# One-hot vectors weighted by their gates on ScalarE instead of VectorE, in an encoder block with dense and sparse expert retrieval

## What is computed

```python
def peer_ffn(x, w_pq, sub_keys1, sub_keys2, peer_u, peer_v):
    ...
    v1, i1 = lax.top_k(s1, PEER_TOPK)
    v2, i2 = lax.top_k(s2, PEER_TOPK)
    ...
    top_s, pos = lax.top_k(cand_s, PEER_TOPK)
    idx = jnp.take_along_axis(cand_i, pos, axis=-1)
    gate = jax.nn.softmax(top_s, axis=-1).astype(x.dtype)
    ...
        u_sel = jnp.take(peer_u, ib, axis=0)
        act = jax.nn.gelu(jnp.einsum('thkd,td->thk', u_sel, xb), approximate=False) * gb
        v_sel = jnp.take(peer_v, ib, axis=0)
        return jnp.einsum('thk,thkd->td', act, v_sel)
```

## Time and profile before

| what | value |
|---|---|
| median of 3 runs | 3290.34 us (3289.21 to 3291.01) |
| profiled execution, its own time | 3295.16 us |
| its span in the profile | 3293.5 us |
| PE busy | 3119.8 us (95%) |
| DVE busy | 2073.9 us (63%) |
| ACT busy | 367.9 us (11%) |
| POOL busy | 682.0 us (21%) |
| mean DMA rate over the span | 313 GB/s |

### The profile page before, as it was taken

One profiled execution on the slowest core, in us unless ns is written; L12 is line 12 of the kernel. 1 busy time (PEld: TensorE's weight loads), 2 busy tenths in 40 slices (PEclk: granted clock), 3 DMA queues, 4 the chain that ended last, 5 costly groups with the idle time before them and its releaser, 6 DMA issues.

```text
span 3293.5 us, 27033 instructions
## 1 busy us (share of the span) xinstructions
PE 3119.8 (95%) x10342; PEld 1889.4 (57%) x10342; DVE 2073.9 (63%) x2874; ACT 367.9 (11%) x653; POOL 682.0 (21%) x557
## 2 busy tenths in 40 slices
PE   8999998899999898999989999999999999999797
PEld 5444443334445577678874447884458853478443
DVE  5356532342668779889997766656566666656675
ACT  1233212320101211112210000000000000000000
POOL 0000000000021134322222333222222333223240
PEclk9999999999999999999999999999999999999899
DMA  6222221047797678998998999999999999999985
GB/s 267 77 77 70 86 65 44 10 166 261 294 408 309 258 316 358 417 387 305 350 350 350 389 422 421 421 415 417 421 421 421 419 419 416 422 421 421 412 368 233
DMA packets 152515, 1029.69 MB, mean 313 GB/s; under 512 B 16464, under 2 KB 21712, under 8 KB 35664
## 3 DMA queue, kind: packets, MB, share of 16 engines
q0 software_dynamic: 78512, 557.88, 41.6%
q1 hardware_dynamic: 73888, 470.24, 36.4%
HBM read 1007.08 MB, written 20.97 MB: 312 GB/s over the span
## 4 chain that ended last, share of the span: by engine, by line
DMA 41%; PE 33%; DVE 18%; issue 4%; ACT 2%; POOL 2%; DVEq 0%; SPq 0%; ACTq 0%; POOLq 0%
DMA arena<-peer_v,arena 40%; PE ps L693 10%; DVE arena L1750 7%; PE ps L1077 4%; PE ps L845 3%; DVE arena L1788 2%; DVE arena L1739 2%; PE ps L935 2%; PE ps L863 2%; PE ps L770 1%; PE ps L1050 1%; PE ps L799 1%; ACT arena L1117 1%; POOL arena L611 1%; PE ps L785 1%
## 5 line engine op out<-in xcount | busy, mean ns | idle before, releaser
L1077 PE MATMUL ps<-arena 128*128 128x512 f32 x2048 | 884.8, 595 | 52.8 <-DVE arena L1800 52.0
L1050 PE MATMUL ps<-arena 128*128 128x256 f32 x4096 | 898.3, 381 | 9.6 <-ACT arena L1333 8.9
L1050 PEld LDWEIGHTS ps<-arena 128*128 128x128 f32 x4096 | 778.7, 191 | 118.9 <-ACT arena L1333 9.7
L1750 DVE SCALAR_TENSOR_TENSOR arena<-arena 128x2048 f32<-128x2048 f32 x256 | 601.8, 2351 | 298.8 <-DMA arena<-peer_v,arena 233.1
L1739 DVE CUSTOM_DVE_ANT_0 arena<-arena 128x2048 f32<-128x2048 f32 x256 | 586.2, 2290 | 288.4 <-DMA arena<-peer_u,arena 286.8
L1077 PEld LDWEIGHTS ps<-arena 128*128 128x128 f32 x2048 | 390.6, 191 | 544.8 <-issue 490.6
L611 POOL DMA_INDIRECT arena<-peer_u,arena x256 | 346.8, 1354 | 1108.3 <-DVE arena L1739 909.3
L622 POOL DMA_INDIRECT arena<-peer_v,arena x256 | 309.2, 1208 | 755.0 <-DVE arena L1750 725.8
L693 PE MATMUL ps<-arena 128*128 128x512 f32 x800 | 345.2, 592 | 1.1 <-ACT arena L1117 1.1
L693 PEld LDWEIGHTS ps<-arena 128*128 128x128 f32 x800 | 151.9, 190 | 192.2 <-issue 192.2
L1117 ACT ACTIVATE arena<-ps 128x512 f32<-128x512 f32 (+3 forms) x247 | 145.2, 611 | 774.9 <-PE ps L855 138.8
(11 more groups left out here) (179 smaller groups left out, 1804.9 us busy)
## 6 DMA issues: line engine op xcount, KB each, us to landing
arena<-peer_ut SPq DMA_DIRECT2D x128, 1024.0 KB
arena<-peer_vt SPq DMA_DIRECT2D x128, 1024.0 KB
arena<-w_row SPq DMA_DIRECT2D x52, 1024.0 KB
arena<-w_mix SPq DMA_DIRECT2D x48, 1024.0 KB
arena<-w_once SPq DMA_DIRECT2D x74, 512.0 KB, 3.5
arena<-w_feat SPq DMA_DIRECT2D x20, 1024.0 KB
dense_gates<-arena SPq DMA_DIRECT2D x8, 2048.0 KB, 7.3
arena<-dense_gates POOLq DMA_DIRECT2D x11, 1024.0 KB, 24.2
```

The lines of the kernel that those rows point to most:

```text
L1050: last = pe.matmul(ps[:, (e // 2) % 4, (e % 2) * DT:(e % 2 + 1) * DT], w[:, kt * P:(kt + 1) * P], XTD[:, kt * DT:(kt + 1) * DT], start=(kt ...
L1077: last = pe.matmul(bank(4 + (c % 2) * 2 + tb), G[:, t * DT + tb * P:t * DT + (tb + 1) * P], w[:, i * 512:(i + 1) * 512], start=(t == 0), s ...
L1750: dve.scalar_tensor_tensor(out=acc, in0=VB[e], scalar=AV[r // 4 % 2][:, r % 4:r % 4 + 1], in1=acc, op0=ALU.mult, op1=ALU.add).then_inc(v_f ...
```

## The change

The multiplication by the gates goes from one VectorE instruction (128x512) to four ScalarE instructions (128x128 each, in place, with one token's column of gates as the scale of each partition). VectorE's comparison now signals a new semaphore `hots_found`, and ScalarE signals `hots_ready`. ScalarE's list has the groups 0 and 1 ahead of the stage, and group n+2 right behind `stage_gates(n)`. VectorE no longer waits for its own comparison.

```diff
@@ one-hot stage, semaphores
-        hots_ready, oh_mm = sem("hots_ready"), sem("oh_mm")
+        hots_found, hots_ready, oh_mm = sem("hots_found"), sem("hots_ready"), sem("oh_mm")
@@ ScalarE
+            def gate_hots(n):
+
+                act.wait_ge(hots_found, n + 1)
+                for i in range(4):
+                    hot = OH[n % 2][:, i * NK:(i + 1) * NK]
+                    t = 2 * DT + 4 * n + i
+                    last = act.activation(hot, hot, ACT.Copy, scale=TB[:, t:t + 1])
+                last.then_inc(hots_ready, 1)
@@ ScalarE, the stage
             t = ONEHOT_FROM // 2 * 2 - 2
+            gate_hots(0)
+            gate_hots(1)
             for n in range(DT // 4):
                 if n % 8 == 1:
                     gelu_dense(0, t)
@@
                 stage_gates(n)
+                if n + 2 < DT // 4:
+                    gate_hots(n + 2)
@@ VectorE, one_hot_vectors
-                link(dve.tensor_tensor(oh, IOTA.unsqueeze(1).unsqueeze(1).broadcast_to([P, 2, 4, NK]),
-                                       turn[:, 0:2, here].unsqueeze(3).broadcast_to([P, 2, 4, NK]), ALU.is_equal))
-                dve.tensor_tensor(oh[:, 0], oh[:, 0], turn[:, 2, here].unsqueeze(2).broadcast_to([P, 4, NK]), ALU.mult
-                                  ).then_inc(hots_ready, 1)
+                dve.tensor_tensor(oh, IOTA.unsqueeze(1).unsqueeze(1).broadcast_to([P, 2, 4, NK]),
+                                       turn[:, 0:2, here].unsqueeze(3).broadcast_to([P, 2, 4, NK]), ALU.is_equal
+                                  ).then_inc(hots_found, 1)
```

## The result

| | before | with the change |
|---|---|---|
| median | 3290.34 us (3282.57 to 3291.51, 5 runs) | 3305.83 us (3303.49 to 3307.11, 5 runs) |
| ratio | | 1.0048, 95% interval 1.0035 to 1.0061 |
| profiled execution, its time | 3295.16 us | 3303.49 us |
| its span | 3293.5 us | 3301.8 us |
| first comparison | 1486.7 | 1474.8 |

The kernel became slower by 15.5 us, 0.48%. The forecast was 8.4 us slower and the range held the time. The lower half of the table tells more than the medians: behind the stage the two executions are alike to 0.3 us in each part, and in the stage the changed kernel loses **19.9 us**. That the spans differ by only 8.3 comes from the part ahead of the stage, which the change doesn't touch.

A forecast was written before the change was run, and what follows sets the result against it. VectorE was taken to bound the one-hot stage. Removing its multiplications gave -26.7 us, stalls and slow clock behind seven stores +35.1, together +8.4: 3298.7 us against the median of 3290.34, range 3282 to 3312.

The forecast's parts named there:

- VectorE sets the pace; below it lies TensorE at 5.24 us for a half tile: One-hot stage: VectorE bounds each half cycle at 6.01 us; TensorE allows no less than 5.24.
- 26.7 us less without stalls: One-hot stage: with 64 multiplications off VectorE, its list ends at 165.5 us against 192.25, if nothing else comes.
- The new instruction: ScalarE's 256 small weightings: 0.295 us from start to start, 0.40 for the last, 1.28 for four.
- TensorE waits 2.9 and 1.15 us behind each store: Groups 10 and 11 wait for weights behind ScalarE's store wait; with slower restarts 4.3 us per store, 30 in all.
- The clock adds 0.65 us per store: TensorE behind each store: half clock after 2.9 us idle loses 1.7 us, about 1.0 of it in the second wait.
- The sum: Whole kernel: -26.7 us from VectorE and +35.1 from seven stores at 5.0 give +8.4 us.
- x at the end of the stage is x at the end of the kernel: Behind the one-hot stage: transfers move the same bytes, so a stage ending x later ends the kernel x later.
- TensorE's lead: At the first product with `peer_v`: of TensorE's 9.5 us ahead of VectorE about 7 are left.
- The clock held: Rival, behind the stores: stalls come but the clock does not fall, or costs nothing; +3.4 us, 3294; chance 0.24.
- The sooner store: Rival: ScalarE resumes under about 6.8 us after a store's issue instead of 7.42; 3280 to 3284 us; chance 0.14.
- The case without stall: Rival: ScalarE gets the weights of groups 10 and 11 out in time, nobody waits behind the store; 3264 us; chance 0.03.
- The median: Whole kernel: the forecast +8.4 us against the median of 3290.34 gives 3298.7 us.

The follow-up runs named there:

- clock held: Changed kernel, but TensorE makes filling products, six and two, before the two groups it waits for behind a store; ratio to before 1.0035.
- another order: Changed kernel, but at groups 8, 16, ... 56 ScalarE weights groups n+2 and n+3 before it waits for the store; 3275.43 us, ratio to before 0.9949.
- second execution: Changed kernel profiled again without any edit; 3319.30 us.
- row late: Changed kernel with two groups weighted before each store wait, and VectorE's dot product of groups 17, 33, 49 made two groups later; ratio to before 0.9966.
- two on VectorE: Changed kernel, but the two groups behind each store (14 of 64) are weighted on VectorE as before; ratio to before 0.9980.

## Why the prediction was right, and where its sizes were off

- *VectorE sets the pace; below it lies TensorE at 5.24 us for a half tile.* Right. Wherever no store is in the way, the changed kernel runs at 5.24 (1523.30 to 1528.54, for one), and so do most half tiles of the others.
- *26.7 us less without stalls.* Too much by 3.2. I let TensorE begin the first pair 2.6 us after the first comparison, when the vectors are ready. But it stands in the middle of tile 18 and begins 5.87 us after it, 1474.84 to 1480.71 in the profile above, and already 1486.67 to 1492.54 in the earlier trace rows, where I had not looked. The term measures 23.5.
- *The new instruction.* 0.295 us from start to start and 0.40 for the last was forecast from the nearest form. It measures 390 ns, and four take 1.26 to 1.28 us. The Trainium skill (VectorE: DVE Perf Modes, section on the TRN2 errata) says that the latency of reading SBUF is paid between instructions, by small tiles once each. Read as "nothing overlaps", that does not hold here at 128 elements: four would take 1.56.
- *TensorE waits 2.9 and 1.15 us behind each store.* Measured 2.69 to 2.91 at the first group. At the second it is 0.97 behind the first two stores, where the clock was still high; in the others the slow clock covers it. The store landed after 7.39 to 7.62 us, nearly as before. With the clock held a store costs 4.27 us, the forecast 4.3.
- *The clock adds 0.65 us per store.* This is the step that failed in size. It adds 1.9. I took 3.4 us at half speed from the one place in the earlier trace rows, and let 1.0 of the loss vanish in the second wait. From the third store on 1.0 did vanish there, but the clock stayed at 0.50 for over 6 us, so the time behind the second wait was slow as well: the group after it lost 0.92 and the half tile 1.19, 2.1 together, with nothing to hide them. Behind the first two stores the clock was low for the forecast 3.4 us, but it fell only as the second wait ended, so next to nothing was hidden, and 1.5 and 1.7 us were lost.
- *The sum.* -23.5 + 7 x 6.2 = +19.9, and 19.9 is measured. Forecast -26.7 + 35.1 = +8.4. So 3.2 of the missing 11.5 are the start, 8.3 the clock. Line 1674 comes 19.9 us later in the stage, not 8.
- *x at the end of the stage is x at the end of the kernel.* Right in the pair of the result: 1568.1 and 1568.2 us behind the first product with `peer_v`. Over all eleven traces that part is 1568.1 to 1572.4 us, so the rule is good to 4 us, not to 0.1. TensorE's lead there fell to 7.2, as worked out.
- *The rivals.* The clock held behind none of the seven stores. The sooner store did not come: landing was 7.39 or more. The case without stall, which I left at 0.03 as excluded by the order, is what another order reaches in five of seven stores.
- *The median.* It moved by 15.5, less than the stage's 19.9, and nearer to the forecast by scatter outside the stage: that is luck. With 19.9 it would be 3310.2, still in the range, but near its end of 3312, and the single second execution, 3319.30, is outside. The argument had the direction and the place right, and under half of the size.

## What to carry to other kernels

Before work goes to an engine with time to spare, ask what that engine waits for in its own order, and who will stand behind that wait. Here 42 us of work in 194 said that ScalarE was free, while it was blocked for 7.4 us at each store. Giving it work that another engine needs soon put the store on the path, and the order of two statements was worth 29 us, three times the 9 that the move gained in the better order. When an idle time of TensorE comes newly about, price the slow clock behind it by the longest that a trace shows, not by one example, and count as hidden only what is sure to come before the next wait ends.

## What the runs showed that I had not expected

- After idle times of 2.7 to 2.9 us the clock stayed low for some 3.4 us behind the first two stores and for over 6 behind the other five, in the same pattern of work. In the second trace it was over 6 behind all seven. Behind the waits of up to 1.81 us in "row late", and of up to 1.97 us in "clock held", it stayed at 1.00, but in "two on VectorE" it fell behind one of 1.38. So the length of the idle time alone does not tell.
- A store of 2 MB landed after 7.4 to 7.5 us in all 14 stores of the two traces of the kernel before, and after 10 to 13.5 at times once TensorE kept its pace and the gathers came every 5.2 us, at a mean of only 350 GB/s. Holding back the loads of weights did not help the late ones.
- Two executions of the same program differ by 11 us ahead of the stage, most of it before 700 us, and by 0.1 to 0.8 in the stage. A comparison of stages by trace told apart what the medians of up to 12 runs left blurred.
